# Position biases enter the attention scores first, as two fp32r matmuls

## The reference, cut to what matters

```python
diff = qi[:, None] - kj[None, :]                       # distance of query and key
bias = table[t5_bucket(diff)]                          # depends on diff and the head alone
s = einsum('qd,sd->qs', q, k) * HEAD_DIM ** -0.5
s = where(valid, s + bias, NEG_INF)                    # swa: 0 <= diff < 128, else diff >= 0
p = exp(s - m) ; p = p / sum(p)                        # swa has a sink in m and in the sum
o = einsum('qs,sd->qd', p, v)
```

## Time and profile before

| | |
|---|---|
| median of 3 runs | 2350.24 us (2349.01 to 2364.05) |
| profiled execution, first to last instruction (its own time; nothing else is shown around it) | 2350.7 us |
| busy in it: TensorE / weight loads / VectorE / ScalarE / GpSimd | 2253.0 / 2157.6 / 1709.2 / 1179.9 / 91.5 us |
| mean granted TensorE clock | 0.982 |
| moved by DMA | 405.11 MB, 172 GB/s |

### The profile page before, as it was taken

The page is one execution under the profiler, slowest core; times in us unless marked ns, Lnnn a source line. Parts: engine busy times, 40 slices in busy tenths (PEclk is TensorE's granted clock), DMA queues, the critical chain, the costliest instruction groups (busy, mean ns, idle before and its releaser), DMA issues.

```text
span 2350.7 us, 43895 instructions
## 1 busy us (share of the span) xinstructions
PE 2253.0 (96%) x18003; PEld 2157.6 (92%) x18003; DVE 1709.2 (73%) x2733; ACT 1179.9 (50%) x1843; POOL 91.5 (4%) x86
## 2 busy tenths in 40 slices
PE   6998999999999999989999999999999989999998
PEld 6976899999999997889998999999997889998998
DVE  6666887997665798887655765765898887656764
ACT  2565445774544533555544544544543555635543
POOL 1000000110010000000000010010000000000110
PEclk8998999999999999999999999999999999999999
DMA  8634575668566653345553666666653345463764
GB/s 240 203 103 138 160 235 188 192 194 251 162 201 187 209 178 109 118 135 179 162 180 108 206 194 193 173 205 188 202 180 108 117 135 179 145 197 104 219 178 137
DMA packets 399911, 405.11 MB, mean 172 GB/s; under 512 B 18182, under 2 KB 392312, under 8 KB 399713
## 3 DMA queue, kind: packets, MB, share of 16 engines
q1 hardware_dynamic: 396177, 389.27, 54.7%
q0 software_dynamic: 3536, 13.04, 1.8%
HBM read 401.17 MB, written 1.09 MB: 171 GB/s over the span
## 4 chain that ended last, share of the span: by engine, by line
PE 71%; DVE 19%; ACT 5%; issue 4%; DMA 1%; DVEq 0%; POOL 0%; ACTq 0%; POOLq 0%
PE gemm_ps L964 46%; PE gemm_ps L967 16%; DVE weights_lo L1594 6%; DVE x_res L2060 4%; PE misc_ps L1106 2%; PE misc_ps L1105 2%; DVE mod_partial L1693 1%; ACT weights_hi L1221 1%; ACT e L1388 1%; DVE h_lo L1732 1%; PE misc_ps L1138 1%; PE misc_ps L1102 1%; DVE neg_max L1820 1%; DVE y L1768 1%; PE misc_ps L1123 1%
## 5 line engine op out<-in xcount | busy, mean ns | idle before, releaser
L1594 DVE TENSOR_TENSOR weights_lo<-raw_weights,weights_hi 128x1024 fp32r<-128x1024 f32 x704 | 836.2, 1199 | 372.9 <-ACT weights_hi L1221 369.6
L1221 ACT CAST weights_hi<-raw_weights 128x1024 fp32r<-128x1024 f32 x704 | 717.0, 1032 | 619.7 <-PE gemm_ps L964 426.5
L964 PE MATMUL gemm_ps<-h_hi,weights_hi 128*128 128x256 f32 x3280 | 927.7, 283 | 11.6 <-DVE h_lo L1732 3.6
L964 PE MATMUL gemm_ps<-h_lo,weights_hi 128*128 128x256 f32 x3280 | 913.1, 278 | 0.0
L964 PE MATMUL gemm_ps<-h_hi,weights_lo 128*128 128x256 f32 x3280 | 912.9, 278 | 0.0
L964 PEld LDWEIGHTS gemm_ps<-h_hi,weights_hi 128*128 128x128 f32 x3280 | 620.0, 189 | 19.1 <-issue 12.7
L964 PEld LDWEIGHTS gemm_ps<-h_lo,weights_hi 128*128 128x128 f32 x3280 | 620.7, 189 | 2.6 <-issue 2.2
L964 PEld LDWEIGHTS gemm_ps<-h_hi,weights_lo 128*128 128x128 f32 x3280 | 620.6, 189 | 0.0
L2060 DVE SCALAR_TENSOR_TENSOR x_res<-zp,param_cols,x_res 128x256 f32<-128x256 f32 x480 | 196.8, 480 | 0.0
L967 PE MATMUL gemm_ps<-weights_hi,hidh 128*128 128x256 f32 x688 | 189.9, 276 | 0.0
L967 PE MATMUL gemm_ps<-weights_hi,hidl 128*128 128x256 f32 x688 | 189.9, 276 | 0.0
(11 more groups left out here) (326 smaller groups left out, 3134.6 us busy)
## 6 DMA issues: line engine op xcount, KB each, us to landing
raw_weights<-in_ffn_w_dram SPq DMA_DIRECT2D x256, 512.0 KB, 4.4
raw_weights<-in_w_in_dram SPq DMA_DIRECT2D x200, 512.0 KB, 3.9
raw_weights<-in_w_mod_dram SPq DMA_DIRECT2D x48, 512.0 KB, 5.0
raw_weights<-in_w_up_dram SPq DMA_DIRECT2D x44, 512.0 KB, 4.6
raw_weights<-in_xattn_kv_dram SPq DMA_DIRECT2D x32, 512.0 KB, 4.4
raw_weights<-in_w_out_dram SPq DMA_DIRECT2D x24, 512.0 KB, 4.5
raw_weights<-in_w_down_dram SPq DMA_DIRECT2D x20, 512.0 KB, 4.8
raw_weights<-in_w_branch_dram SPq DMA_DIRECT2D x16, 512.0 KB, 4.6
```

What stands on the lines that cost most here:

```text
L964: mm = pe.matmul(ps[:, c, 0:T], w[:, m, kt, c * P:(c + 1) * P], x[:, f, :], start=start, stop=stop_)
L1221: act.copy(unit_of(WH, m % SPLIT, u), unit_of(RAWB, u["raw"] % RAW, u)).then_inc(sems["weights_rounded"], 1)
L1594: dve.tensor_tensor(unit_of(WL, m % SPLIT, u), unit_of(RAWB, u["raw"] % RAW, u), unit_of(WH, m % SPLIT, u), ALU.subtract).then_inc(sems["w ...
```

## The change

The bias lines are split once, at the start, into an fp32r high half (`lines_hi`, by ScalarE's copies) and the rest (`lines_lo`, by three subtractions on VectorE in a new step `bias_rest`, placed just before the first weight splits). Both are written to the scratch and both are read back as shifted copies, so each load of bias rows has a second half. `FLIP` is fp32r and loaded on GpSimd's queue at the start instead of SP's. In a call, the bias matmuls come first: for each map, high half and rest, each for both query tiles; then the four query-key matmuls, still float32, in the order tile 0 map 0, tile 0 map 1, tile 1 map 0, tile 1 map 1. They wait for queries and keys only then. The rest halves live in space that is free at that time (`gl`; half of `gh` and the old place of `qa`; `tmp2`), which adds a late load for moba's heads 4 to 7 and a wait in the split of `ob`.

```diff
+    add("bias_rest")
     for m in range(AHEAD):
         add("presplit", m=m)
...
         split("G", "oa", "qa", fts=4)
+        add("hankel_late", after=("split", "G", "oa", 3))
...
+    FLIP = sb("flip", [P, P], F32R)
...
-                sp.dma_start(FLIP[:], a["flip"]).then_inc(sems["consts_in"], 16)
...
             if c["hname"] is not None:
-                pe.wait_ge(sems["hankel_in"], at(*c["hname"]))
+                pe.wait_ge(sems["flip_in"], at("flip"))
+                pe.wait_ge(sems["hankel_late_in" if c["hname"] == ("hank_late",) else "hankel_in"], at(*c["hname"]))
+                for m in range(c["maps"]):
+                    for n, part in enumerate(c["hank"][m]):
+                        for qt in range(2):
+                            nk = P * (qt + 1)
+                            pe.matmul(scores_at(c, qt, m, nk), FLIP[:], part[:, T - nk:T], start=n == 0 and qt == 0, stop=False, skip_group_check=True)
             if k["cfg"] in ("swa", "moba"):
                 pe.wait_ge(sems["vec_norm"], at("qk", ...))
...
-                        pe.matmul(ps, c["q"][m][:, qt * P:(qt + 1) * P], c["k"][m][:, 0:nk], start=True, stop=False)
-                        mm = pe.matmul(ps, FLIP[:], c["hank"][:, c["head"][m], T - nk:T], start=False, stop=True)
+                        mm = pe.matmul(ps, c["q"][m][:, qt * P:(qt + 1) * P], c["k"][m][:, 0:nk], start=False, stop=True, skip_group_check=True)
...
             for i in range(3):
-                act.copy(o_set["lines"][:, i, :], PB[0:8, i, 0:LINE]).then_inc(sems["act_setup"], 1)
-                act.wait_ge(sems["act_setup"], up("act_setup", ("lines_read",)))
+                act.copy(o_set["lines_hi"][:, i, :], PB[0:8, i, 0:LINE]).then_inc(sems["act_setup"], 1)
+                up("act_setup", ("lines_hi",))
...
+            if k["gen"] == "ob" and f == 4:
+                act.wait_ge(sems["pe_attn"], at("scores", "moba", 1))
...
+        def vec_bias_rest(k):
+            dve.wait_ge(sems["act_setup"], at("lines_hi"))
+            for i in range(3):
+                dve.tensor_tensor(o_set["lines_lo"][:, i, :], PB[0:8, i, 0:LINE], o_set["lines_hi"][:, i, :], ALU.subtract).then_inc(sems["vec_setup"], 1)
+                up("vec_setup", ("lines_lo",))
...
-            dve.wait_ge(sems["line_out"], at("lines_out"))
             for f in range(NF):
+                if f == NF - 1:
+                    dve.wait_ge(sems["line_out"], at("lines_out"))
...
+            pool.dma_start(FLIP[:], a["flip"]).then_inc(sems["flip_in"], 16)
...
+        def pool_bias_rest(k):
+            pool.wait_ge(sems["act_setup"], at("lines_hi"))
+            pool.dma_start(scratch[0].rearrange("i h j -> h i j"), o_set["lines_hi"][:]).then_inc(sems["line_out"], 16)
+            up("line_out", by=16)
+            pool.wait_ge(sems["vec_setup"], at("lines_lo"))
+            pool.dma_start(scratch[1].rearrange("i h j -> h i j"), o_set["lines_lo"][:]).then_inc(sems["line_out"], 16)
             up("line_out", ("lines_out",), by=16)
+
+        def bias_rows(dst, part, which, first, n, reached, sem="hankel_in"):
+            src = bass.AP(tensor=scratch.tensor, offset=((part * 3 + which) * 8 + first) * LINE, ap=[[1, P], [LINE, n], [1, T]])
+            pool.dma_start(dst, src).then_inc(sems[sem], 16)
+            up(sem, reached, by=16)
...
+            bias_rows((o_m["hank2"] if which == 2 else o_b1["hank1"])[:], 0, which, 0, 8, None)
+            if which == 0:
+                bias_rows(o_b1["gl"][:], 1, which, 0, 8, reached)
+            if which == 1:
+                bias_rows(o_b1["gh"][:, 4:8, :], 1, which, 0, 4, reached)
+            if which == 2:
+                bias_rows(o_m["hank2_rest"][:], 1, which, 0, 8, reached)
                 pool.dma_start(o_m["win"][:], a["windows"]).then_inc(sems["windows_in"], 16)
```

More of the change, by code:

```diff
@@ L624, in build @@
     CC, SP4, QG = sb("silu_c", [P, NF]), sb("softplus4", [P, NF]), sb("qk_gains", [P, 4])
-    ONES, IDENT, FLIP, HEADS = (sb(n, [P, P]) for n in ("ones", "ident", "flip", "headsum"))
+    ONES, IDENT = (sb(n, [P, P]) for n in ("ones", "ident"))
+    FLIP = sb("flip", [P, P], F32R)
+    HEADS = sb("headsum", [P, P])
     EPS = sb("eps", [P, 4])
@@ L741, in unit_of, with bias_of @@
         return wide[:, 0:u["nkt"], :]
+    def bias_of(cfg, h):
+        if cfg == "swa":
+            return o_b1["hank1"][:, h, :], o_b1["gl"][:, h, :]
+        if cfg == "moba":
+            return o_b1["hank1"][:, h, :], o_b1["gh"][:, 4 + h, :] if h < 4 else o_b1["hank_late"][:, h - 4, :]
+        return o_m["hank2"][:, h, :], o_m["hank2_rest"][:, h, :]
     def att(cfg, i):
@@ L751, in att @@
                         v=[[v[:, b, vcol(m):vcol(m) + HD] for b in (0, 1)] for m in (0, 1)],
-                        hank=o_b1["hank1"], head=[2 * i, 2 * i + 1], E=o_b1["e1"][:, i % 2], PT=o_b1["pt1"], o=q[:, i, :],
-                        causal=True, pack="pair", hname=("hank", 0 if cfg == "swa" else 1, 0))
+                        hank=[bias_of(cfg, 2 * i), bias_of(cfg, 2 * i + 1)], E=o_b1["e1"][:, i % 2], PT=o_b1["pt1"], o=q[:, i, :],
+                        causal=True, pack="pair", hname=("hank", 0, 0) if cfg == "swa" else ("hank", 1, 0) if i < 2 else ("hank_late",))
         l = int(cfg[-1])
@@ L2110, in vec_mem_turn @@
             up("vec_norm", ("memf", f"l{k['l']}", half))
-        parts = dict(setup=vec_setup, params=vec_params, turn_x=vec_turn_x, mod=vec_mod, mod_sum=vec_mod_sum, adapt=vec_adapt, split=vec_split,
+        parts = dict(setup=vec_setup, bias_rest=vec_bias_rest, params=vec_params, turn_x=vec_turn_x, mod=vec_mod, mod_sum=vec_mod_sum, adapt=vec_adapt, split=vec_split,
                      residual=vec_residual, evac_ytok=vec_ytok, update_x=vec_update_x, row_wide=vec_row_wide, rstd_cols=vec_rstd_cols, evac_qk=vec_evac_qk, qk_norm=vec_qk_norm,
@@ L2159, in pool_hankel, with pool_hankel_late @@
                 pool.wait_ge(*done(k["after"]))
[L2160 to L2164 removed]
+            which, reached = k["which"], ("hank", k["which"], k["l"])
+            bias_rows((o_m["hank2"] if which == 2 else o_b1["hank1"])[:], 0, which, 0, 8, None)
[5 more added lines that the diff above has]
+                bias_rows(o_m["hank2_rest"][:], 1, which, 0, 8, reached)
                 pool.dma_start(o_m["win"][:], a["windows"]).then_inc(sems["windows_in"], 16)
                 up("windows_in", ("win", k["l"]), by=16)
+        def pool_hankel_late(k):
+            pool.wait_ge(*done(k["after"]))
+            bias_rows(o_b1["hank_late"][:], 1, 1, 4, 4, ("hank_late",), "hankel_late_in")
         def pool_blocks(k):
@@ L2198, in pool_mem_load @@
             up("mem_in", ("memt", k["l"]), by=16)
-        parts = dict(setup=pool_setup, bias=pool_bias, hankel=pool_hankel, gain=pool_gain, mem_load=pool_mem_load, hid_split=pool_hid_split, pads1=pool_blocks)
+        parts = dict(setup=pool_setup, bias_rest=pool_bias_rest, hankel=pool_hankel, hankel_late=pool_hankel_late, gain=pool_gain, mem_load=pool_mem_load, hid_split=pool_hid_split, pads1=pool_blocks)
         for kind, k in steps:
```

28 lines of the change are left out of this document (11 added, 17 removed).

## The result

The change takes 2331.92 us in the median of 4 runs (2324.3 to 2334.33), the kernel before 2355.56 in 4 (2349.01 to 2364.05): a ratio of 0.9887, with a 95% interval from 0.9856 to 0.9919. The profiled execution of the change is its fastest one, 2324.3 us with a span of 2322.5; the one of before had 2350.7, at the same mean granted clock (0.982 both). In the traces the gain is 28.2 us, in the medians 23.6, and the runs of one kernel spread over 10 us.

What follows compares the result with a forecast made beforehand. TensorE was taken to bound most of the chain, with VectorE limiting the mixers. Block 1 13.0, mixers 8.3 and 9.2, FLIP 0.5, less 3 at the start, make 28.0: from 2350.2 to 2322 us, 8-in-10 range 2310 to 2342.

Steps and rivals of the forecast that it cites:

- The change of shape, 0.20 us, eight to one: In each scores call, switching between 64-row and 128-row matmuls costs 0.20 us; eight such switches become one.
- Row halves together: In a call's query-key matmuls, both maps' row halves run side by side: 0.85 us, else 1.50.
- The rival of serial halves: In the query-key matmuls, row halves run one behind the other: 23 us less, 2327 us; chance 0.22.
- the drain stays: In scores calls, regrouping doesn't remove the 0.20 us: 1.2 us saved a call, 2339 us; chance 0.25, shared with VectorE absorbing.
- The bias part, 0.92 us: In each scores call, eight fp32r bias instructions take 0.92 us, with no change of shape in front.
- Mixers, 7.6 to 8.3 and 8.5 to 9.2: Mixers of layers 0 and 1: gains of 7.6 to 8.3 and 8.5 to 9.2 us, limited by VectorE's idle times.
- Block 1, 9.4 to 13.0: Block 1's four swa calls and last moba call gain 9.4 to 13.0 us, after 3 off for the clock.
- The start, 3 us: At the start, one more megabyte of bias rows delays w_in's load: 3 us lost, 1 to 6.
- `FLIP` off SP, -0.5: Taking FLIP off SP's queue lets the modulation load on the chain go 0.5 us sooner.
- The clock rival: At the 16 diff calls, longer TensorE idling lowers the granted clock: 45 us lost, 2367 us; chance 0.05.
- The sum, 28.0: Whole kernel: the terms' short end adds up to 28.0 us saved, the long end to 23.0.

Runs made afterwards that it cites:

- e3: The kernel before, still float32, with each map's bias matmuls then its query-key matmuls, one map after the other: 2335.36 us in one run.
- e2: The whole change with fp32r, but query-key and bias matmuls alternating as in the kernel before: 2356.13 us, ratio 0.9998.
- e8: The change with two of every three convolution multiply-adds on VectorE left out: span 2292.5 us, against 2325.7 for the kernel before with the same cut.
- e6: The change with GpSimd's clearing and loading of block weights held until VectorE's adapted blocks are done: 2329.68 us, ratio 0.9902.
- e1: The kernel before with the new order alone, bias matmuls first, still float32 with one set of bias rows: 2327.67 us, ratio 0.9887.
- e4: The change with its first 2 MB of bias rows asked for behind the first projection's last unit: 2324.9 us, ratio 0.9881.
- e5: The kernel before with the new order alone in float32, and the first bias rows asked for behind the first projection: 2322.98 us, ratio 0.9874.

## Why the prediction was right, and where it was off

- **The change of shape, 0.20 us, eight to one.** The price is right, the count isn't: it is eight to two (table under e3). I looked in the earlier trace rows for the cost of the change back to the unit and found none, but no call before ends with a change. e2, with eight changes and fp32r, keeps 3.60 us a call. The statement of the Trainium skill, "TensorEngine Tiling (Array Packing)", Key Properties, that a change of tiling mode drains TensorE, agrees that such a change costs something.
- **Row halves together.** Right: eight instructions take what four of one half take, 0.86 and 0.85. The rival of serial halves falls, and so does *the drain stays*.
- **The bias part, 0.92 us.** Right: its four pairs start 0.23 us apart. The 1.01 us to the first query-key instruction hold 0.1 of the change of shape. The whole call saves 4.16 - 1.97 = 2.2 us instead of 2.4, by the change that I didn't count.
- **Mixers, 7.6 to 8.3 and 8.5 to 9.2.** 8.7 and 10.2, above both. The way to it was right, the idle times of VectorE as credit, and e8 shows the bound by lifting it. What I hadn't named is how the bound looks: not a later call, but an idle TensorE between a call and its unit, 0.4 to 4.4 us, since VectorE's evacuation stands behind its softmax. The fifth call gives nothing at all.
- **Block 1, 9.4 to 13.0.** At a step of GpSimd in the first block's feed-forward part, behind all its calls, the change is 5.5 us ahead (434.59 against 440.11); with the start's 3.8 to 4.8 added that is 9.3 to 10.3, the lower end. That nothing holds these calls back was wrong: behind the third and fourth swa call and the third moba call TensorE now waits 1.39, 1.59 and 1.97 us for VectorE's copy of a value product (L1898), where it waited for none before. The third swa call takes 3.33 us instead of 4.08. Against that the first one ran at full clock (granted 1.00 from 144 to 148 us, 0.50 before).
- **The start, 3 us.** The mis-sized term: 4.8 us at the fourth unit, 3.8 at the thirteenth. The place was right, w_in's load comes late. The price wasn't: I took one megabyte at 329 GB/s, and e6 shows that the second megabyte alone costs 0.9 us at most. With the second megabyte in front, the block weights' load, which I had named and not priced, is asked for at 53.71 instead of 50.80, just where w_in's begin at 54.02; asked for later (e6) it costs nothing. The held VectorE instruction I hadn't foreseen; it costs nothing on top.
- **`FLIP` off SP, -0.5.** Not seen: the step behind the modulation starts at 49.96 us, and did so at 49.84 before.
- **Between the mixers** I forecast nothing, and 3.6 us came. They are no work saved. They fall in the stretch right behind the first mixer, from the eighth call's turn to the next load of `gain_c`: 169.9 us before and 166.3 in the change. The same stretch in layer 1 takes 166.9 before, 167.2 in the change and 170.1 in e6, which has the new order too. Where it is long the granted clock is lower in its two parts: 0.98 and 0.99 in layer 0 before, 0.98 and 0.98 in e6's layer 1, against 0.99 and 1.00 in the change's layer 0. So the difference is a fall of the clock that one execution has and another hasn't. Before and e2 have it in layer 0; that the old order brings it on there isn't excluded, but layer 1 doesn't show it.
- **The clock rival** didn't come: the mean granted clock is 0.982 in both traces, and in the two mixers 0.99 and 0.98 in both. The runs of the change spread over 10 us, and their mean clocks (0.974 to 0.982) don't put them in order; why the median lies 7.6 us above the profiled execution stays open.

The sum, 28.0, met the traces' 28.2 by luck: 5.0 us too much up to the end of block 1 (0.8 to 1.8 of it the start, 0.5 `FLIP`, the rest block 1's calls), 1.4 too little in the mixers and 3.8 too little elsewhere, of which 3.6 are the clock between the mixers. Without these the traces give 24.6 us, and the medians 23.6.

## What to carry to other kernels

Count changes of array shape as you count instructions, the way back included: grouping matmuls of one shape, which also lets row halves stand next to each other, gave all of this gain, a cheaper data type for half of them none that can be seen. When a stage is that near to a second engine, price a shorter call by what that engine has standing in front of the next unit, in its order, and expect the move of filler work away from there to cost more elsewhere than it frees. Before adding a load, see which other loads it pushes in front of the next one that TensorE needs. And before you put the cost down to an instruction that is visibly held, look at a trace in which it isn't.

## What the runs showed of the hardware that I had not expected

VectorE's `tensor_scalar` on 128 x 8 values needs 0.17 us alone. When GpSimd's work had begun before it, it mostly ended just when that did:

| kernel | GpSimd busy until | tensor_scalar from, us | to |
|---|---|---|---|
| before | clearing, 50.50 | 50.05, 0.48 | 50.53 |
| e1 | clearing, 50.99 | 50.28, 0.75 | 51.03 |
| change | two row loads issued, then clearing, 53.41 | 50.17, 3.28 | 53.45 |
| e6 | second row load issued, 51.23 | 50.73, 0.50 | 51.23 |
| e8 | second row load issued, then clearing, 52.57 | 50.27, 2.33 | 52.60 |
| e2 | row loads issued from 50.31 on | 50.29, 0.17 | 50.46 |
| e4 | clearing, 50.64 | 50.66, 0.17 | 50.83 |

VectorE's other instructions keep their length beside the same clearing (before: a split of two inputs, 1.22 us, and a sum read from PSUM, 0.17). In the change it was not let in between three GpSimd instructions in a row. In e2 it started 0.02 us before the issuing and wasn't held. And issuing a load doesn't always hold it: in e5 it took its 0.17 us at 51.35, between 50.66 and 52.05, when GpSimd issued two block loads. The Trainium skill, "SBUF — State Buffer", Who interferes with whom, has the rule: VectorE and GpSimd share a pair of ports as an exclusive lock, `tensor_scalar` is among the operations that can take it, and whoever issues second blocks for the whole of the other's instruction. The rows of the table agree; e5's case the rule does not explain; that one VectorE instruction waits for several of GpSimd's is this case's addition.

And the listed length of a float32 matmul group doesn't tell whether the array's halves work side by side; the start of what follows does, if nothing else holds it: the eight query-key instructions are listed with 0.93 us in every call, whether the next unit came after 0.86 or after 1.58.
